# One more feed-forward layer in pairs, an earlier last chunk, and one weight sum on GpSimd

## The chip, the cores and the metric

One NeuronCore of a Trainium2 chip runs the whole network in one launch. The metric is the device time of one execution in microseconds, as the median of several runs.

## The reference

The input x is one sequence of 256 tokens with 1024 features. It passes through 13 stages: eight feed-forward layers (FFN 0 to 7) and between them four mixers (HGRN, forgetting attention, short convolution, NSA attention) and one stage that makes shared keys and values for NSA. All is float32. An FFN, which is what the change touches most, is

```python
def swiglu(h, w_in, w_out):
    gate, up = jnp.split(h @ w_in, 2, axis=-1)
    return (jax.nn.silu(gate) * up) @ w_out
# x = x + 0.5 * swiglu(rmsnorm(x), w_in, w_out), w_in 1024 x 5632, w_out 2816 x 1024
```

The shared keys and values include compressed ones: windows of 32 tokens plus a position vector, through a small two-layer network. NSA needs them, and a table of relative position biases.

## The kernel before

**Split products.** A float32 product is made of fp32r matmuls of high and low parts: hi*hi + lo*hi + hi*lo, three matmuls of 512 columns for each 128 rows of the contraction. ScalarE (ACT) makes the high part of every weight block by a copy to fp32r (lines 599, 1022, 1131), VectorE (DVE) the low part by subtracting it (lines 609, 1030, 1266). A block is 128x2048 (1 MB). TensorE (PE) does nothing but products and transposes.

**An FFN** is worked in 11 chunks of 256 hidden features (FC). For each chunk the input product (gate and up), silu and the product by DVE, a transposition of the result ("turn"), and the output product ("second"), which adds into four PSUM banks acc 0 to 3 over all chunks (bank a holds token tile a // 2, column half a % 2).

**Pairs.** In FFN 0 two and in FFN 1, 2, 3, 4 and 7 three pairs of chunks (table PAIRED, line 78; 17 pairs in all) take a Strassen-like form: seven products B11, B21, T2, T3, T1, B22, T4 of 12 matmuls each (pe_pair, line 849) in place of eight. T1 to T4 use sums of weight blocks: T3 = b12 + b22, made by a DMA of POOL's queue that adds while it loads; T2 = b11 + T3 into b11; T4 = b21 + T2 into b21; T1 = T2 - b22, over b11 (dve_block_sum, line 1033: sums at lines 1047, 1051, 1056). The last three are DVE's, and the semaphore st_add counts them in the order T2, T4, T1. Each sum is then split like any block. DVE's order in the first pair of an FFN is: split B11, output weights of the chunk before, read, turn, split B21, read, sum T2, sum T4, split T2, sum T1, split T3, split T1, split B22, split T4. In the other pairs: split B11, turn and output weights, read, sum T2, split B21, read, sum T4, split T2, sum T1, turn, output weights, split T3, and on. "Read" is silu(gate) * up (line 1332), with one operand in PSUM.

**The last chunk** (10) of an FFN: PE does second(9) in two halves, each followed by the transposes of one half of chunk 10 (line 999), and then second(10) with the half of the hidden features outside and the banks inside, so that all four banks end within the last twelve matmuls (lines 976 to 1000). ACT and DVE split its output weights into the usual tiles wo_hi and wo_lo half by half, once second(9) has freed them (lines 1237 to 1410). In paired FFNs these weights are loaded early into a place of their own (raw_last; the list ASIDE). DVE then adds the four banks to x (line 1415).

**Stage borders.** A mixer transposes x by a product with a diagonal matrix that holds 1/rms of each token: ACT squares x, DVE and ACT make the root and the reciprocal, DVE the diagonal (line 767), PE the product (line 674). An FFN after an FFN transposes x (line 676) and scales later.

**Around FFN 5.** FFN 5 is not paired; in its arena room POOL prepares the kv stage (pool_kv, line 2222): bias table, two 1 MB weight loads, and a sum over the 32 positions in 47 small instructions (line 2249), which PE uses in FFN 6 (line 2346). PE makes the product of the bias table in FFN 5 (pe_bias_slot, line 2287).

**What sets the order.** Every engine's program is written out by hand in one fixed order, with semaphores between them. SP issues the loads, in its own fixed order; a place is loaded again when the low part of what it held is made.

## Time and profile before

| what | us |
|---|---|
| median of 3 runs (2092.23 to 2093.51) | 2092.26 |
| the profiled execution, by the same clock as the runs | 2089.7 |
| span of its trace, first to last instruction | 2088.4 |
| PE busy | 2038.8 |
| DVE busy | 1512.6 |
| ACT busy | 1138.7 |
| POOL busy | 93.1 |

The mean granted TensorE clock was 0.996 of the full one. A busy share is an average over stages of different kinds; PE's ends are modelled, so its records overlap (a matmul of 512 columns has a record of 0.39 us and the next starts 0.23 later). In a timeline row, the bracket gives the idle time of the engine just before, and what ended it.

### The profile page before, as it was taken

What the parts mean: (1) busy time and instruction counts of PE and PEld (TensorE: products, weight loads), DVE (VectorE), ACT (ScalarE), POOL (GpSimd) and SP (SyncE); (2) the same over time, 40 slices, a digit from 0 to 9 for tenths busy, and PEclk for the clock granted to TensorE, in tenths of its full rate; (3) what the DMA queues carried; (4) which work ended last, traced back from release to release, by engine and by line L of the source; (5) the groups of instructions that cost most, each with busy time, mean ns of one, the idle gap of its engine ahead of it and who ended that gap; (6) DMA issues with size and microseconds to landing.
All of it is one profiled execution on the core that took longest, in us unless ns stands there. A gap on an engine that the chain in (4) does not pass through costs nothing.

```text
span 2088.4 us, 26202 instructions
## 1 busy us (share of the span) xinstructions
PE 2038.8 (98%) x10287; PEld 1705.6 (82%) x10287; DVE 1512.6 (72%) x1777; ACT 1138.7 (55%) x1417; POOL 93.1 (4%) x130
## 2 busy tenths in 40 slices
PE   8999999999999999999999999999999999989999
PEld 6887988888888778888888879888888887877887
DVE  6885687997898676698789866655555555767995
ACT  6555436555665558665566543544455444765653
POOL 2000000000000000000000000007001000000000
PEclk9999999999999999999999999999999999989999
DMA  9644426877265452687736545685637654117562
GB/s 278 237 154 150 162 82 219 259 247 241 102 222 183 143 172 73 207 260 250 238 112 211 193 141 181 194 240 185 192 131 183 202 194 164 68 42 241 182 222 81
DMA packets 232955, 377.82 MB, mean 181 GB/s; under 512 B 18766, under 2 KB 129786, under 8 KB 232832
## 3 DMA queue, kind: packets, MB, share of 16 engines
q1 hardware_dynamic: 220896, 351.56, 49.4%
q0 software_dynamic: 10992, 22.78, 6.2%
q10 hardware_dynamic: 944, 1.79, 0.3%
q8 instruction: 82, 1.34, 0.3%
q14 instruction: 41, 0.34, 0.0%
HBM read 374.53 MB, written 1.57 MB: 180 GB/s over the span
## 4 chain that ended last, share of the span: by engine, by line
PE 86%; DVE 7%; ACT 4%; issue 2%; DMA 1%; DVEq 0%; ACTq 0%; SPq 0%
PE bank L584 11%; PE bank L586 11%; PE bank L585 11%; PE acc L930 6%; PE acc L932 6%; PE acc L931 6%; PE bank L863 3%; PE bank L862 3%; PE bank L864 3%; PE tr L862 2%; PE tr L863 2%; PE bank L579 2%; PE tr L864 2%; PE bank L580 2%; PE bank L581 2%
## 5 line engine op out<-in xcount | busy, mean ns | idle before, releaser
L609 DVE TENSOR_TENSOR w_lo_<-raw_in,w_hi_ 128x2048 fp32r<-128x2048 f32 (+1 forms) x265 | 418.7, 1589 | 134.8 <-ACT w_hi_ L599 134.5
L584 PE MATMUL bank<-w_hi_,xt_hi_ 128*128 128x512 f32 x1104 | 444.1, 402 | 4.0 <-DVE xt_lo_ L710 2.4
L586 PE MATMUL bank<-w_hi_,xt_lo_ 128*128 128x512 f32 x1104 | 431.3, 391 | 0.0
L585 PE MATMUL bank<-w_lo_,xt_hi_ 128*128 128x512 f32 x1104 | 430.2, 390 | 0.0
L599 ACT ACTIVATE w_hi_<-raw_in 128x2048 fp32r<-128x2048 f32 (+1 forms) x265 | 351.2, 1346 | 76.4 <-DMA raw_in<-ffn_w_in 26.5
L1266 DVE TENSOR_TENSOR wo_lo_<-raw_out,wo_hi_ 128x2048 fp32r<-128x2048 f32 x80 | 183.5, 2293 | 195.1 <-ACT wo_hi_ L1131 195.0
L1030 DVE TENSOR_TENSOR w_lo_<-arena,w_hi_ 128x2048 fp32r<-128x2048 f32 x119 | 270.8, 2284 | 4.8 <-ACT w_hi_ L1022 4.8
L1022 ACT ACTIVATE w_hi_<-arena 128x2048 fp32r<-128x2048 f32 x119 | 225.6, 1910 | 40.8 <-DVE arena L1047 19.8
L584 PEld LDWEIGHTS bank<-w_hi_,xt_hi_ 128*128 128x128 f32 x1104 | 207.7, 188 | 45.9 <-issue 4.8
L586 PEld LDWEIGHTS bank<-w_hi_,xt_lo_ 128*128 128x128 f32 x1104 | 207.2, 188 | 44.8
L1131 ACT ACTIVATE wo_hi_<-raw_out 128x2048 fp32r<-128x2048 f32 x80 | 153.0, 1912 | 163.2 <-PE acc L932 123.1
L585 PEld LDWEIGHTS bank<-w_lo_,xt_hi_ 128*128 128x128 f32 x1104 | 208.0, 188 | 38.2
L930 PE MATMUL acc<-wo_hi_,ht_hi_ 128*128 128x512 f32 x576 | 225.5, 391 | 0.8 <-DVE ht_lo_ L1261 0.8
L932 PE MATMUL acc<-wo_hi_,ht_lo_ 128*128 128x512 f32 x576 | 224.5, 390 | 0.0
L931 PE MATMUL acc<-wo_lo_,ht_hi_ 128*128 128x512 f32 x576 | 224.2, 389 | 0.0
L930 PEld LDWEIGHTS acc<-wo_hi_,ht_hi_ 128*128 128x128 f32 x576 | 108.1, 188 | 25.1 <-issue 1.4
L932 PEld LDWEIGHTS acc<-wo_hi_,ht_lo_ 128*128 128x128 f32 x576 | 108.1, 188 | 22.7
L931 PEld LDWEIGHTS acc<-wo_lo_,ht_hi_ 128*128 128x128 f32 x576 | 108.2, 188 | 22.2
L1172 ACT ACTIVATE silu_<-bank,rstd_ 128x256 f32<-128x256 f32 x108 | 51.0, 473 | 129.2 <-PE bank L586 129.1
L1126 ACT ACTIVATE ht_hi_<-tr 128x512 fp32r<-128x512 f32 x80 | 47.5, 593 | 123.9 <-PE tr L911 110.9
L579 PE MATMUL bank<-xt_hi_,w_hi_ 128*128 128x256 f32 x352 | 101.9, 289 | 2.8 <-DVE xt_lo_ L770 2.8
L580 PE MATMUL bank<-xt_lo_,w_hi_ 128*128 128x256 f32 x352 | 99.6, 283 | 0.0
(438 smaller groups left out, 3415.0 us busy)
## 6 DMA issues: line engine op xcount, KB each, us to landing
raw_in<-ffn_w_in SPq DMA_DIRECT2D x216, 512.0 KB, 5.3
raw_out<-ffn_w_out SPq DMA_DIRECT2D x82, 1024.0 KB, 5.1
arena<-ffn_w_in SPq DMA_DIRECT2D x68, 1024.0 KB, 7.5
arena<-ffn_w_in POOLq DMA_DIRECT2D x17, 1024.0 KB, 14.0
raw_in<-hg_w_in SPq DMA_DIRECT2D x16, 1024.0 KB, 5.1
raw_in<-fox_w_in SPq DMA_DIRECT2D x16, 1024.0 KB, 5.4
raw_in<-conv_w_in SPq DMA_DIRECT2D x12, 1024.0 KB, 5.1
arena<-ffn_w_out SPq DMA_DIRECT2D x6, 1024.0 KB, 7.1
```

The lines of the kernel that those rows point to most:

```text
L584: mm(o, xt_hi[:, k, tok], wh(k)[:, 0:w], start=first, stop=False)
L585: mm(o, xt_hi[:, k, tok], wl(k)[:, 0:w], start=False, stop=False)
L586: last = mm(o, xt_lo[:, k, tok], wh(k)[:, 0:w], start=False, stop=end)
L599: act.e.activation(g.piece(g.wh, n, half, k), raw, ACT.Copy).then_inc(g.w_hi, 4 if k is None else 1)
L609: dve.e.tensor_tensor(g.piece(g.wl, n, half, k), raw, g.piece(g.wh, n, half, k).bitcast(F32), ALU.subtract).then_inc(g.w_lo, 4 if k is Non ...
L930: mm(o, g.hth[:, at, :], g.oh[:, i, cols], start=(c == 0 and i == 0), stop=False)
L931: mm(o, g.hth[:, at, :], g.ol[:, i, cols], start=False, stop=False)
L932: ins = mm(o, g.htl[:, at, :], g.oh[:, i, cols], start=False, stop=False)
L1022: act.e.activation(g.wh[:, op % 4], g.block_of(i), ACT.Copy).then_inc(g.w_hi, 4)
L1030: dve.e.tensor_tensor(g.wl[:, op % 4], g.block_of(i), g.wh[:, op % 4].bitcast(F32), ALU.subtract).then_inc(g.w_lo, 4)
L1131: act.e.activation(g.oh[:], g.raw_out[:], ACT.Copy).then_inc(g.wo_hi, 2)
L1266: dve.e.tensor_tensor(g.ol[:], g.raw_out[:], g.oh[:].bitcast(F32), ALU.subtract).then_inc(g.wo_lo, 2)
```

## The change

FFN 5 gets three pairs like FFN 1. The output weights of the last chunk are loaded in two halves into xg and a piece of the arena, and (except in FFN 6) split early into the tile that held the split sums of x. PE makes both halves' transposes after the first half of second(9), and goes through second(10) bank by bank, so that the banks end one after the other; before an FFN, the transposes of the first token tile come ahead of bank 3. DVE's additions to x are split up accordingly: before a mixer banks 2 and 3 are added behind the first diagonal. The sum T4 of each pair (b21 + T2, 128x2048) is made by GpSimd, behind its loading DMA, in place of DVE. POOL's preparation for the kv stage starts at the end of FFN 5, and the bias product moves into the kv stage.

The changed lines, cut to those that the text speaks of (the bias product's move and the last calls are left out):

```diff
@@ -75,7 +75,7 @@
-PAIRED = {f: (2, 5, 8) if f else (4, 7) for f in (0, 1, 2, 3, 4, 7)}
+PAIRED = {f: (2, 5, 8) if f else (4, 7) for f in (0, 1, 2, 3, 4, 5, 7)}
@@ -117,7 +117,7 @@
-ASIDE = [m_of(f, NCH - 1) for f in PAIRED]
+ASIDE = [m_of(f, NCH - 1) for f in range(8)]
@@ -276,11 +276,19 @@
-        self.raw_last = self.area(10240, FC // P, D)
+        self.raw_last = [self.area(8768 if f == 6 else CW, D) for f in range(8)]
-    def last_out(self, f):
-        return self.raw_last if f in PAIRED else self.raw_out
+    def last_out(self, f, i):
+        return self.raw_last[f] if i else self.xg[:].rearrange("p a b -> p (a b)")
+    def last_split(self, f):
+        if f == 6:
+            return self.oh, self.ol
+        return [self.sums_split[:, i].rearrange("p a b c -> p (a b c)").rearrange("p (i n) -> p i n", n=D)
+                for i in range(2)]
@@ -345,7 +353,7 @@
-        self.pe_w1 = [self.area(8768, 2, P), self.area(9792, 2, P)]
+        self.pe_w1 = [self.area(13120, 2, P), self.area(13376, 2, P)]
@@ -473,9 +481,13 @@
-                if f in PAIRED and c == NCH - 1:
-                    sp.wait_ge(g.prod, PDN[N0[s] + PAIRED[f][-1]] + 6)
-                    sp.e.dma_start(g.raw_last, w_out[c]).then_inc(g.last_in, 16)
+                if c == NCH - 1:
+                    if f == 6:
+                        sp.wait_ge(g.kv_hidden, 1)
+                    else:
+                        sp.wait_ge(g.prod, PDN[N0[s] + PAIRED[f][-1]] + 6)
+                    for half in range(2):
+                        sp.e.dma_start(g.last_out(f, half), w_out[c][:, half]).then_inc(g.last_in, 16)
@@ -765,6 +777,9 @@
+        if t == 0:
+            for a in (2, 3):
+                dve_ffn_add(g, dve, S_FFN.index(s - 1), a)
@@ -779,6 +794,8 @@
+            if s and STAGES[s - 1] == "ffn" and not t and not half:
+                dve_ffn_add(g, dve, S_FFN.index(s - 1), 3)
@@ -895,7 +912,7 @@
-        pe_turn_x(g, pe, s)
+        pe_turn_x(g, pe, s, first=int(s > 0 and STAGES[s - 1] == "ffn"))
@@ -973,31 +989,40 @@
-    for c in (NCH - 2, NCH - 1):
-        for i in range(FC // P):
-            if c == NCH - 2:
-                pe.wait_ge(g.ht_lo, 12 * f + c + 1)
...
+    def last_second(i, a, oh, ol, end):
+        t, cols = a // 2, slice(a % 2 * CW, (a % 2 + 1) * CW)
+        at, mm, o = i * NT + t, pe.e.matmul, g.accs[a][:]
+        mm(o, g.hth[:, at, :], oh[:, i, cols], start=False, stop=False)
+        mm(o, g.hth[:, at, :], ol[:, i, cols], start=False, stop=False)
+        return mm(o, g.htl[:, at, :], oh[:, i, cols], start=False, stop=end)
+    c = NCH - 2
+    pe.wait_ge(g.ht_lo, 12 * f + c + 1)
+    pe.wait_ge(g.wo_lo, 2 * m_of(f, c) + 2)
+    for i in range(FC // P):
+        for a in range(4):
+            ins = last_second(i, a, g.oh, g.ol, False)
+        ins.then_inc(g.second, 1)
+        if i:
+            continue
+        for t in range(NT):
+            pe.wait_ge(g.h, 22 * f + 2 * (NCH - 1) + t + 1)
+        for half in range(FC // P):
+                ins = pe.e.transpose(g.tr[half][:, t * P:(t + 1) * P], g.h_[:, t, half * P:(half + 1) * P], g.ident[:])
+    c = NCH - 1
+    oh, ol = g.last_split(f)
+    for a, i in ([(a, i) for i in range(FC // P) for a in range(4)] if f == 6 else
+                 [(a, i) for a in range(4) for i in range(FC // P)]):
+        if (a, i) == (3, 0) and s + 1 in S_FFN:
+            for half in range(2):
+                pe_turn_half(g, pe, s + 1, 0, half)
+        pe.wait_ge(g.ht_lo, 12 * f + c + i + 1)
+        pe.wait_ge(g.wo_lo, 2 * m_of(f, c) + i + 1)
+        ins = last_second(i, a, oh, ol, i == 1)
+        if i == 1:
+            ins.then_inc(g.acc, 1)
@@ -1045,10 +1070,6 @@
-    elif i == T4:
-        dve.wait_ge(g.w_lo, 4 * (op + B21) + 4)
-        dve.wait_ge(g.st_add, 3 * p + 1)
-        dve.e.tensor_tensor(b21, b21, b11, ALU.add).then_inc(g.st_add, 1)
@@ -1063,6 +1084,10 @@
+            b11, b21 = g.blocks[0], g.blocks[2]
+            pool.wait_ge(g.w_lo, 4 * (OPN[N0[S_FFN[f]] + c] + B21) + 4)
+            pool.wait_ge(g.st_add, 3 * p + 1)
+            pool.e.tensor_tensor(b21, b21, b11, ALU.add).then_inc(g.st_add, 1)
@@ -1235,13 +1260,16 @@
+    oh = g.last_split(f)[0]
+    act.wait_ge(g.last_in, 32 * (f + 1))
+    if f != 6:
+        act.wait_ge(g.prod, PDN[n0 + PAIRED[f][-1]] + 6)
+        for i in range(FC // P):
+            act.e.activation(oh[:, i], g.last_out(f, i), ACT.Copy).then_inc(g.wo_hi, 1)
-        if f in PAIRED:
-            act.wait_ge(g.last_in, 16 * (list(PAIRED).index(f) + 1))
-        else:
-            act.wait_ge(g.landed_out, 16 * outs_until(m_of(f, c)))
-        act.e.activation(g.oh[:, i], g.last_out(f)[:, i], ACT.Copy).then_inc(g.wo_hi, 1)
+        if f == 6:
+            act.e.activation(oh[:, i], g.last_out(f, i), ACT.Copy).then_inc(g.wo_hi, 1)
@@ -1355,7 +1383,6 @@
-                dve_block_sum(g, dve, p, T4)
@@ -1369,7 +1396,6 @@
-                dve_block_sum(g, dve, p, T4)
@@ -1401,19 +1427,31 @@
+    oh, ol = g.last_split(f)
+    def last_low(i):
+        dve.wait_ge(g.wo_hi, 2 * m_of(f, c) + i + 1)
+        dve.e.tensor_tensor(ol[:, i], g.last_out(f, i), oh[:, i].bitcast(F32), ALU.subtract).then_inc(g.wo_lo, 1)
+    if f != 6:
+        for i in range(FC // P):
+            last_low(i)
-        dve.wait_ge(g.wo_hi, 2 * m_of(f, c) + i + 1)
-        dve.e.tensor_tensor(g.ol[:, i], g.last_out(f)[:, i], g.oh[:, i].bitcast(F32), ALU.subtract).then_inc(g.wo_lo, 1)
+        if f == 6:
+            last_low(i)
-    for t in range(NT):
-        for half in range(2):
-            cols, a = slice(half * CW, (half + 1) * CW), 2 * t + half
-            dve.wait_ge(g.acc, 4 * f + a + 1)
-            dve.e.scalar_tensor_tensor(g.x[:, t, cols], g.accs[a][:], 0.5, g.x[:, t, cols], ALU.mult,
-                                       ALU.add).then_inc(g.x_new, 1)
+    for a in range(3 if s + 1 in S_FFN else 4 if s + 1 == len(STAGES) else 2):
+        dve_ffn_add(g, dve, f, a)
+def dve_ffn_add(g, dve, f, a):
+    t, cols = a // 2, slice(a % 2 * CW, (a % 2 + 1) * CW)
+    dve.wait_ge(g.acc, 4 * f + a + 1)
+    dve.e.scalar_tensor_tensor(g.x[:, t, cols], g.accs[a][:], 0.5, g.x[:, t, cols], ALU.mult, ALU.add).then_inc(g.x_new, 1)
@@ -1505,7 +1543,7 @@
-    pool.wait_ge(g.wo_lo, 2 * NCH)
+    pool.wait_ge(g.acc, 4)
@@ -2221,10 +2259,14 @@
-    for i in range(4):
-        pool.wait_ge(g.x_new, 4 * X[S_FFN[5] - 1] + i + 1)
+    pool.wait_ge(g.prod, PDN[N0[S_FFN[5]] + PAIRED[5][-1]] + 7)
+    pool.wait_ge(g.landed_out, 16 * outs_until(m_of(5, NCH - 2)))
+    pool.wait_ge(g.last_in, 32 * 6)
+    pool.e.dma_start(g.onehot[0:REL_ROWS], t["c_rel"]).then_inc(g.rel_in, 16)
+    for kv, w in enumerate((t["cmp_w1_k_2"], t["cmp_w1_v_2"])):
+        pool.e.dma_start(g.w1[kv * DH:(kv + 1) * DH], w.rearrange("(j d) h -> d j h", d=DH)).then_inc(g.compress_in, 16)
+    pool.wait_ge(g.acc, 4 * 6)
-    pool.e.dma_start(g.onehot[0:REL_ROWS], t["c_rel"]).then_inc(g.rel_in, 16)
@@ -2233,15 +2275,13 @@
-    for kv, w in enumerate((t["cmp_w1_k_2"], t["cmp_w1_v_2"])):
-        pool.wait_ge(g.prod, PDN[N0[S_FFN[5]] + 3 + kv])
-        pool.e.dma_start(g.w1[kv * DH:(kv + 1) * DH], w.rearrange("(j d) h -> d j h", d=DH)).then_inc(g.compress_in, 16)
+    pool.e.memset(g.kv0, 0.0).then_inc(g.kv_set, 1)
+    pool.wait_ge(g.kv_set, 6)
+    pool.e.memset(g.vv.rearrange("p a b g d -> p (a b g) d")[:, :, DH:], 1.0).then_inc(g.kv_set, 1)
+    pool.wait_ge(g.kv_set, 7)
-    pool.e.memset(g.kv0, 0.0).then_inc(g.kv_set, 1)
-    pool.wait_ge(g.kv_set, 7)
-    pool.e.memset(g.vv.rearrange("p a b g d -> p (a b g) d")[:, :, DH:], 1.0).then_inc(g.kv_set, 1)
@@ -2342,7 +2381,7 @@
-        pe.wait_ge(g.kv_set, 6)
+        pe.wait_ge(g.kv_set, 8)
@@ -3151,6 +3192,7 @@
+    pool_pairs(g, pool, 5)
```

## Rows read from the trace of the kernel before

**Rows 1.** The page's part 1: busy us, share of the span, instructions.

```profile
PE 2038.8 (98%) x10287; PEld 1705.6 (82%) x10287; DVE 1512.6 (72%) x1777; ACT 1138.7 (55%) x1417; POOL 93.1 (4%) x130
```

**Rows 2.** Waits of PE, longest kind first: total us, times, longest.

```profile
PE tr L674 <- DVE diag_ L767: 8.9, 5, 1.8
```

**Rows 3.** Timeline of PE, products B22 and T4 of FFN 1's first pair.

```profile
399.49 0.39 PE L862 MATMUL bank<-w_hi_,sums_split 128*128 128x512 f32 x1
...
402.72 0.47 PE L862 MATMUL tr<-w_hi_,xt_hi_ 128*128 128x512 f32 x1 [0.28 <-DVE w_lo_ L1030]
```

**Rows 4.** Timeline of PE, FFN 1 and FFN 5: start us, us, instruction.

```profile
354.22 0.38 PE L676 MATMUL tr<-ident,x_tok 128*128 128x128 f32 x2
...
535.64 0.39 PE L990 MATMUL acc<-wo_hi_,ht_lo_ 128*128 128x512 f32 x1
...
1339.83 0.38 PE L676 MATMUL tr<-ident,x_tok 128*128 128x128 f32 x2
...
1528.97 0.39 PE L990 MATMUL acc<-wo_hi_,ht_lo_ 128*128 128x512 f32 x1
```

**Rows 5.** The chain that ended last, near 1349: start us, us, what.

```profile
1348.65 0.96 PE acc L2292 x2
```

**Rows 6.** Timeline of POOL, where the sum over positions begins.

```profile
1412.19 0.61 POOL L2254 TENSOR_TENSOR arena<-arena,gains 128x256 f32<-128x256 f32 x1 [9.25 <-DMA arena<-cmp_w_v]
```

**Rows 7.** Timeline of DVE, then of POOL, near 1448.

```profile
1448.08 2.72 DVE L609 TENSOR_TENSOR w_lo_<-raw_in,w_hi_ 128x2048 fp32r<-128x2048 f32 x1 [0.68 <-ACT w_hi_ L599]
...
1448.04 0.61 POOL L2254 TENSOR_TENSOR arena<-arena,gains 128x256 f32<-128x256 f32 x1
1448.73 2.39 POOL L2261 TENSOR_TENSOR arena<-arena 128x128 f32<-128x128 f32 x1
```

**Rows 8.** Timeline of PE, the product with the sum over positions.

```profile
1591.89 0.28 PE L2346 MATMUL acc<-arena 128*128 128x2 f32 x2
```

**Rows 9.** Timeline of DVE, then of PE, from FFN 0 into the mixer.

```profile
194.63 1.38 DVE L1415 SCALAR_TENSOR_TENSOR x_tok<-acc,x_tok 128x512 f32<-128x512 f32 x2 [1.05 <-PE acc L990]
...
198.42 0.35 PE L674 MATMUL tr<-diag_,x_tok 128*128 128x128 f32 x1 [1.78 <-DVE diag_ L767]
```

**Rows 10.** Timeline of DVE, then of ACT, first pair of FFN 1.

```profile
383.22 2.29 DVE L1051 TENSOR_TENSOR arena<-arena 128x2048 f32<-128x2048 f32 x1
385.43 2.28 DVE L1030 TENSOR_TENSOR w_lo_<-arena,w_hi_ 128x2048 fp32r<-128x2048 f32 x1
...
396.21 2.28 DVE L1030 TENSOR_TENSOR w_lo_<-arena,w_hi_ 128x2048 fp32r<-128x2048 f32 x1
...
383.21 1.92 ACT L1022 ACTIVATE w_hi_<-arena 128x2048 fp32r<-128x2048 f32 x1 [2.81 <-DVE arena L1047]
```

**Rows 11.** Groups of POOL by form: count | busy us, mean ns | idle before.

```profile
L3003 POOL TENSOR_TENSOR arena<-silu_ 128x128 f32<-128x128 f32 x16 | 7.3, 456 | 264.1 <-DVE silu_ L2913 264.1
...
L2283 POOL COPY arena<-arena 128x240 f32<-128x240 f32 x1 | 0.6, 607 | 0.0
...
L2283 POOL COPY arena<-arena 128x112 f32<-128x112 f32 x1 | 0.4, 382 | 18.0 <-DMA arena<-bias_rows 18.0
```

**Rows 12.** Timeline of DVE, second pair of FFN 1, then of FFN 2.

```profile
423.58 2.28 DVE L1030 TENSOR_TENSOR w_lo_<-arena,w_hi_ 128x2048 fp32r<-128x2048 f32 x1
...
428.38 2.28 DVE L1030 TENSOR_TENSOR w_lo_<-arena,w_hi_ 128x2048 fp32r<-128x2048 f32 x1
...
433.56 2.28 DVE L1266 TENSOR_TENSOR wo_lo_<-raw_out,wo_hi_ 128x2048 fp32r<-128x2048 f32 x1
...
614.82 2.28 DVE L1266 TENSOR_TENSOR wo_lo_<-raw_out,wo_hi_ 128x2048 fp32r<-128x2048 f32 x1
```

**Rows 13.** Timeline of PE, where each of those two output parts is used.

```profile
437.02 0.40 PE L930 MATMUL acc<-wo_hi_,ht_hi_ 128*128 128x512 f32 x1
...
618.69 0.40 PE L930 MATMUL acc<-wo_hi_,ht_hi_ 128*128 128x512 f32 x1
```

More of the change, by code:

```diff
@@ L677, in pe_turn_half, with pe_turn_x @@
     ins.then_inc(g.turned, 1)
-def pe_turn_x(g, pe, s):
-    for t in range(NT):
+def pe_turn_x(g, pe, s, first=0):
+    for t in range(first, NT):
         for half in range(2):
@@ L914, in second @@
     def second(c):
-        if c == 0 and f == 5:
+        if c == 0 and f == 6:
             pe.wait_ge(g.kv_rows, 1)
-        elif c == 0 and f == 6:
             pe.wait_ge(g.kv_gelu, 2)
@@ L998, in pe_ffn @@
-            for t in range(NT):
-                ins = pe.e.transpose(g.tr[i][:, t * P:(t + 1) * P], g.h_[:, t, i * P:(i + 1) * P], g.ident[:])
+                ins = pe.e.transpose(g.tr[half][:, t * P:(t + 1) * P], g.h_[:, t, half * P:(half + 1) * P], g.ident[:])
             ins.then_inc(g.h_turned, 1)
+    c = NCH - 1
[10 more added lines that the diff above has]
+            ins.then_inc(g.acc, 1)
@@ L2319, in pe_kv @@
             j = 2 * (c - 1) + t
+            if (c, t) == (1, 0):
+                pe_bias(g, pe)
             if c == 1:
@@ L2366, in read @@
                 return
+            if j == 0:
+                act_bias(g, act)
             if j == 3:
@@ L3100, in pe_program @@
     pe_conv(g, pe)
[L3101 removed]
+    pe_ffn(g, pe, 5)
     pe_kv(g, pe)
```

48 lines of the change are left out of this document (13 added, 35 removed).

## Prediction

> **What bounds the kernel now.** I read the page's busy times first: PE is busy for 2038.8 us of a span of 2088.4 [rows 1]. So all stalls of TensorE together are worth at most 50 us, and a change can win in two ways only: less work for PE, or fewer of those stalls. Then the waits of PE: the largest regular one is at the start of each mixer, where the transposes wait for the diagonal matrix, 8.9 us in five waits [rows 2]. Last the timelines of one FFN, engine by engine. There VectorE (DVE) runs almost without a gap from the split of one weight block to the next, and it comes in just ahead of PE: in the first pair PE already waits 0.28 us for a weight split [rows 3]. What matters for the moved sum is therefore not how much DVE does, but how far ahead of PE each of its splits is.
>
> The profiled execution took 2089.7 us, 2.6 below the median of the three runs (2092.26). I make the sum against the profiled execution and add it to the median.
>
> **Part 1, FFN 5 in pairs.** FFN 1, which has three pairs and also follows a mixer, runs from 354.22 to 535.64 + 0.39 = 536.03, or 181.8 us; FFN 5 without pairs runs from 1339.83 to 1528.97 + 0.39 = 1529.36, or 189.5 us [rows 4]. The difference is 7.7 us. The count agrees: a pair needs 7 x 12 matmuls where two plain chunks need 96, so 3 x 12 = 36 fewer at about 0.23 us each, 8.3 us, less what the pair form loses. The bias product (0.96 us [rows 5]) now sits in FFN 5 and only moves to the kv stage. Term: -7.7 + 0.96 = **-6.8 us**.
>
> What moves with it: POOL's preparation for the compressed keys. Its position sum ran from 1412 [rows 6] to past 1448 [rows 7], some 40 us. Its two 1 MB weight loads now go out near the end of FFN 5, its memsets and two small loads behind the last accumulation, 1529 less 7. Fifteen us for memsets and loads and 40 for the sum end some 7 us before the product that needs it, which came at 1591.89, 62.5 us behind FFN 5's end [rows 8]. I cost it at nothing; if the sum is 15 us longer, the kernel pays 8. The small adds also hold DVE's splits of the kv stage by up to 0.44 us each, as they held those of FFN 5 before, where no wait of PE came of it. SP's block loads and POOL's three more accumulating loads in FFN 5 follow the order of FFN 1, whose stretch contains them.
>
> **Part 2, the last chunk and the stage borders.** The weights of the last chunk are split before the chunk, and the accumulators end one after the other, so the additions to x start sooner. Before, PE stood 1.78 us at a mixer's start [rows 9]: the last addition (0.7, half of the pair of 1.38 [rows 9]) and the chain of statistics to the diagonal (1.1). After, tile 0's diagonal is ready when PE ends. But DVE adds the last two quarters only behind that diagonal, so tile 1's comes two additions (1.4), a square on ScalarE (0.8, an estimate from the additions, of the same size) and the 1.1 later, 3.2 us behind PE's end, where its transposes used to start at 1.78 plus tile 0's own, about 1.95. That wins 0.5 a border. It gives back 0.2, because the second half of the last chunk's activations is now needed after three matmuls instead of twelve. Four borders at -0.3; at the NSA stage FFN 6 keeps its order and only gets the later additions (+0.8); two FFN-FFN borders at -0.1; the end of the kernel, where the last addition follows the same +0.2, +0.3. Term: -1.2 + 0.8 - 0.2 + 0.3 = **-0.3 us**. Nothing in the rows shows this order, so the ends are -5 (most of the 8.9 gone) and +3.
>
> **Part 3, the fourth sum on GpSimd.** It goes from DVE, where it took 2.29 us [rows 10], to POOL, 20 times (17 pairs before, three more in FFN 5). Two things follow: its own length P, and what DVE does meanwhile.
>
> The length. No such add is in the trace. POOL's add of 128 columns took 456 ns; its copies of 112 and 240 columns took 382 and 607 [rows 11], which is 1.76 ns a column above a fixed 0.185. A multiplication of 256 columns with a repeated second operand took 0.61 [rows 6]. Low end: the step from 456 to 610 carried on, 2.8 us. High end: 16 x 456, 7.3 us, as if nothing of an instruction were fixed. The copy's line with a second input can't be under 3.8. I take the add's own row with the copy's fixed part, (456 - 185) / 128 = 2.12 ns a column, so **P = 4.5 us**. The Trainium skill (GPSIMD Engine Reference, section 3.1) gives a measured 4497 ns for this very add and tells authors to leave two-input arithmetic to VectorE; by that figure the sum would be the same.
>
> What DVE does. At 1448.04 a POOL multiply starts; DVE's split starts 0.04 later and takes 2.72 us instead of 2.28; POOL's next add, from 1448.73, takes 2.39 instead of 0.46 [rows 7]. I read this as exclusion: whichever engine started first with two SBUF inputs, the other stood. Then DVE is held not for 0.44 but for all of P. The Trainium skill (SBUF — State Buffer, "Who interferes with whom") says so: an instruction of VectorE with two SBUF inputs and a GpSimd instruction that reads SBUF exclude each other for the whole instruction. The trace shows it only for POOL operations of half a us. With that rule the sum is the one below; without it, it is rival (a).
>
> First pair of an FFN. The fourth sum started at 383.22, right behind the second; ScalarE made the high part of that same second sum in its shadow (383.21, 1.92 us), and DVE's split of it came at 385.43 [rows 10]. After, POOL starts at 383.2, surely first, since DVE has nothing to do until 385.1, and DVE's split starts at 383.3 + P: later by P - 2.13, 2.4 us. Everything DVE does up to the split of B22 follows back to back. That split ended at 396.21 + 2.28 = 398.49 and PE wanted it at 399.49 [rows 3, 10]: 1.0 us is covered. The 0.28 us wait at the next product goes, since its chain starts at PE itself. Loss P - 3.4 = 1.1 us, in seven FFNs (0 to 5 and 7): **+7.6 us**.
>
> Second pair (chunk 5). POOL starts behind the split of B21 (423.58 + 2.28), while DVE reads a PSUM bank, and is ahead again. DVE's next split, at 428.38, starts at 426.05 + P, 2.2 us late. The split of the output weights ended at 433.56 + 2.28 = 435.84, and PE wanted it at 437.02; in FFN 2 at 617.10 and 618.69 [rows 12, 13]. Covered are 1.2 and 1.6 us, so the loss is 1.0 and 0.6, mean 0.85, in six FFNs (1 to 5 and 7): **+5.1 us**. Both losses together grow by 13 us for each us of P: at the high end of 7.3 they would be 49 us, at the low end of 2.8 they are nothing, or at best the seven waits of 0.28 less, -2 us. In the third pair the same split lies further ahead of PE, and I take nothing. DVE's third sum overwrites what the fourth reads and so waits for POOL as well; with the split held, that wait is over when DVE comes to it. SP and POOL: the fourth sum queues behind the accumulating load of its own pair, long landed, and ahead of the next pair's, whose target is not loaded before the third product's split; I take nothing.
>
> **Sum:** -6.8 - 0.3 + 7.6 + 5.1 = **+5.6 us**, 0.27%: 2095.3 for the profiled execution, 2097.9 for the median.
>
> **Rivals.** (a) *Faster: no exclusion over the whole length.* If DVE passes beside a long POOL add, its split runs at 385.1, and only the third sum waits for POOL, until 387.8 at P = 4.5, when it began anyway (385.43 + 2.28). Then part 3 costs nothing and the time is 2092.3 - 7.1 = 2085.2. It decides at the split behind the second sum: 2.3 us long under this rival, about 4.9 under mine. Against it: the 2.72 us [rows 7]. (b) *The add is short.* Exclusion holds but P is 3.8 or less: the losses fall to 0.4 and 0.15 a pair, 3.7 us in all, and the time is 2088.9. Part 3 costs nothing below P = 3.4. (c) *The losses are larger:* P = 5.3 adds 0.8 us to 13 pairs, 10.4 us, 2108; a position sum that holds up the kv stage or FFN 6 would end near there too. (d) *The change doesn't do what it says:* both calls on DVE are gone and FFN 5 is in the table of pairs, so this isn't open; what could be is that FFN 5 gains less, because its block loads meet POOL's 2 MB; that is 1 to 3 us inside the ranges.
>
> **Chances.** My case (P of 4.2 to 4.8, full exclusion) 0.55; (a) 0.15; (b) or losses half as large as read 0.15; (c) 0.15. A change of 0.2%, 4.2 us, is what a measurement of this kernel can tell from none. My own case has its losses known to about 3 us, so it ends above 2096.5 in two of three, and within 0.2% else. Slower 0.48, within 0.2% 0.27, faster 0.25. The range takes in (a) and (c): 2084 to 2108; my case alone is 2094 to 2102.
>
> **What would show it.** In the profile after: POOL rows for a 128x2048 add, 20 of them, near 4.5 us; the split behind the second sum near 4.9 us in first pairs and as long in second pairs; new waits of PE for a weight split (about 1 us, at the products T3 and B22 of first pairs) and for the output weights' low part in second pairs; FFN 5 about 7 us shorter; the waits for the diagonal split into a small one and one of about 1.2 us. If the split stays at 2.3 us, my reading of the exclusion is wrong and the kernel is faster; if POOL's add is 3 us, the price was.

## The result, and the profile after

The changed kernel takes 2111.7 us (median of 4 runs, 2109.1 to 2117.4) against 2092.2 for the kernel before beside it: a ratio of 1.0099, with an interval of [1.0087, 1.0111]. It is slower by 19.5 us. The prediction was 2097.9, between 2084 and 2108. The sign was right, the size was not: 19.5 where 5.6 was forecast, and outside the range.

The profiled execution took 2109.1 us. First the page's part 1 of the changed kernel, to be read against [rows 1]:

```profile
PE 2040.4 (97%) x10251; PEld 1700.7 (81%) x10251; DVE 1586.2 (75%) x1792; ACT 1158.1 (55%) x1421; POOL 186.3 (9%) x153
```

PE has 36 matmuls fewer, as counted. DVE has lost the 2.3 us sum in 17 pairs, and yet it is busy for 74 us more. A part is the work of FFN 5's pairs (run 1 below, without the move, has 1566 us); the rest is time in which DVE's instructions were held, and their records count it as busy. It shows in the groups of instructions, whose columns are the form, the count, the busy time, the mean length in ns, and the idle time before:

```profile
L1055 DVE TENSOR_TENSOR w_lo_<-arena,w_hi_ 128x2048 fp32r<-128x2048 f32 x140 | 384.2, 2752 | 27.3 <-ACT w_hi_ L1047 27.3
...
L1090 POOL TENSOR_TENSOR arena<-arena 128x2048 f32<-128x2048 f32 x20 | 92.3, 4614 | 514.4 <-DVE w_lo_ L1055 261.9 <-DVE arena L1072 252.5
```

GpSimd's sum takes 4.6 us, twenty times. The weight splits of the pairs, which took 2.28 us [rows 10, 12], now take 2.75 in the mean: if 120 of them are as before, the 20 beside POOL's sum are longer by 3.2 us each. In the timeline they are 4.8 us in first pairs, 6.2 to 6.5 in second pairs and 5.1 in third pairs (6.5 in FFN 2's); the prediction had put the second pairs at 4.9 like the first. The waits of PE (total us, times, longest), longest kind first:

```profile
PE bank L879 <- DVE silu_ L1303: 9.4, 7, 2.1
PE tr L928 <- DVE ht_lo_ L1289: 9.2, 8, 1.8
PE acc L686 <- DVE diag_ L779: 6.8, 5, 2.1
```

The first two are new. They are 18.6 us, and PE's idle time as a whole grew by 18 us. Neither is the wait whose cover I had computed (at the product of B22, and at the output weights). My list of signs had named the product T3 too, but for a weight split, not for a read of DVE.

### The profile page after: what moved, and what is told of

It is laid out like the page before. It is cut to its first block, busy times and chain, and to the rows that moved or that the text cites. A ratio compares the mean times of both kernels' runs of the same rounds, so it can differ in the third digit from the quotient of the medians.

```text
span 2107.7 us, 26229 instructions
## 1 busy us (share of the span) xinstructions
PE 2040.4 (97%) x10251; PEld 1700.7 (81%) x10251; DVE 1586.2 (75%) x1792; ACT 1158.1 (55%) x1421; POOL 186.3 (9%) x153
## 4 chain that ended last, share of the span: by engine, by line
PE 80%; DVE 10%; ACT 6%; issue 3%; DMA 0%; DVEq 0%; ACTq 0%; SPq 0%
PE bank L596 10%; PE bank L598 10%; PE bank L597 10%; PE acc L946 6%; PE acc L948 6%; PE acc L947 6%; DVE w_lo_ L1055 3%; PE bank L879 2%; PE bank L880 2%; PE bank L881 2%; PE bank L591 2%; PE tr L879 2%; PE bank L592 2%; PE bank L593 2%; PE tr L880 2%
## 5 line engine op out<-in xcount | busy, mean ns | idle before, releaser
L621 DVE TENSOR_TENSOR w_lo_<-raw_in,w_hi_ 128x2048 fp32r<-128x2048 f32 (+1 forms) x247 | 390.4, 1589 | 128.6 <-ACT w_hi_ L611 128.2
L596 PE MATMUL bank<-w_hi_,xt_hi_ 128*128 128x512 f32 x1008 | 406.2, 403 | 3.8 <-DVE xt_lo_ L722 2.0
L1055 DVE TENSOR_TENSOR w_lo_<-arena,w_hi_ 128x2048 fp32r<-128x2048 f32 x140 | 384.2, 2752 | 27.3 <-ACT w_hi_ L1047 27.3
L598 PE MATMUL bank<-w_hi_,xt_lo_ 128*128 128x512 f32 x1008 | 393.9, 391 | 0.0
L597 PE MATMUL bank<-w_lo_,xt_hi_ 128*128 128x512 f32 x1008 | 392.8, 390 | 0.0
L611 ACT ACTIVATE w_hi_<-raw_in 128x2048 fp32r<-128x2048 f32 (+1 forms) x247 | 327.8, 1347 | 80.5 <-DMA raw_in<-ffn_w_in 31.1
L1047 ACT ACTIVATE w_hi_<-arena 128x2048 fp32r<-128x2048 f32 x140 | 265.6, 1911 | 74.3 <-DVE arena L1077 46.5
L598 PEld LDWEIGHTS bank<-w_hi_,xt_lo_ 128*128 128x128 f32 x1008 | 189.1, 188 | 41.0
L1090 POOL TENSOR_TENSOR arena<-arena 128x2048 f32<-128x2048 f32 x20 | 92.3, 4614 | 514.4 <-DVE w_lo_ L1055 261.9
L947 PEld LDWEIGHTS acc<-wo_lo_,ht_hi_ 128*128 128x128 f32 x576 | 108.2, 188 | 22.2
L879 PE MATMUL bank<-w_hi_,sums_split 128*128 128x512 f32 x240 | 96.9, 404 | 9.4 <-DVE silu_ L1303 9.4
```

The costliest lines, as they stand in the source:

```text
L596: mm(o, xt_hi[:, k, tok], wh(k)[:, 0:w], start=first, stop=False)
L597: mm(o, xt_hi[:, k, tok], wl(k)[:, 0:w], start=False, stop=False)
L598: last = mm(o, xt_lo[:, k, tok], wh(k)[:, 0:w], start=False, stop=end)
L611: act.e.activation(g.piece(g.wh, n, half, k), raw, ACT.Copy).then_inc(g.w_hi, 4 if k is None else 1)
L621: dve.e.tensor_tensor(g.piece(g.wl, n, half, k), raw, g.piece(g.wh, n, half, k).bitcast(F32), ALU.subtract).then_inc(g.w_lo, 4 if k is Non ...
L879: mm(bank[:], hi[:, k], wh[:, k], start=k == 0, stop=False)
```

## Where the held split lands

The first pair of FFN 1, DVE, then POOL, then PE (start us, us, instruction):

```profile
384.36 2.28 DVE L1072 TENSOR_TENSOR arena<-arena 128x2048 f32<-128x2048 f32 x1
388.76 4.82 DVE L1055 TENSOR_TENSOR w_lo_<-arena,w_hi_ 128x2048 fp32r<-128x2048 f32 x1 [2.12 <-ACT w_hi_ L1047]
...
398.08 0.69 DVE L1303 TENSOR_TENSOR silu_<-bank,arena 128x512 f32<-128x512 f32 x1
```
```profile
386.80 4.63 POOL L1090 TENSOR_TENSOR arena<-arena 128x2048 f32<-128x2048 f32 x1 [16.75 <-DVE arena L1072]
```
```profile
398.82 0.50 PE L879 MATMUL bank<-w_hi_,sums_split 128*128 128x512 f32 x1 [1.23 <-DVE silu_ L1303]
399.15 0.40 PE L880 MATMUL bank<-w_lo_,sums_split 128*128 128x512 f32 x1
```

The split is held until POOL is through and then runs: 4.82 us, where I had said 4.9. Everything behind it on DVE is late, and PE stops at the T3 product. This product writes PSUM bank 1, and may do so only when DVE has read the second product out of it. That read is the addition at L1303 (`gate0` in the code), queued behind the split of T3. In the kernel before, the same read and the first matmul of T3 stood like this, DVE and PE:

```profile
392.21 0.69 DVE L1275 TENSOR_TENSOR silu_<-bank,arena 128x512 f32<-128x512 f32 x1
...
393.89 0.39 PE L862 MATMUL bank<-w_hi_,sums_split 128*128 128x512 f32 x1
```

The read ended at 392.90, 1.0 us ahead of PE. This time by which an instruction is ahead of whoever needs it is its cover.

The second pair, DVE, POOL, PE:

```profile
428.42 2.28 DVE L1055 TENSOR_TENSOR w_lo_<-arena,w_hi_ 128x2048 fp32r<-128x2048 f32 x1
...
431.02 6.52 DVE L1055 TENSOR_TENSOR w_lo_<-arena,w_hi_ 128x2048 fp32r<-128x2048 f32 x1
437.63 2.29 DVE L1077 TENSOR_TENSOR arena<-arena 128x2048 f32<-128x2048 f32 x1
439.84 0.68 DVE L1289 TENSOR_TENSOR ht_lo_<-tr,ht_hi_ 128x512 fp32r<-128x512 f32 x1
440.44 2.28 DVE L1294 TENSOR_TENSOR wo_lo_<-raw_out,wo_hi_ 128x2048 fp32r<-128x2048 f32 x1
```
```profile
430.79 4.60 POOL L1090 TENSOR_TENSOR arena<-arena 128x2048 f32<-128x2048 f32 x1 [20.11 <-DVE w_lo_ L1055]
```
```profile
440.58 0.66 PE L928 MATMUL tr<-ident,h_tok 128*128 128x128 f32 x4 [1.60 <-DVE ht_lo_ L1289]
```

PE stops for 1.60 us at the transposes of the middle chunk. They overwrite the bank from which DVE takes the low half of the hidden rows turned before (ht_lo), 0.6 us of work that stands behind the T1 sum. In the kernel before, the T1 sum, ht_lo and the turn stood like this:

```profile
430.75 2.29 DVE L1056 TENSOR_TENSOR arena<-arena 128x2048 f32<-128x2048 f32 x1
432.96 0.68 DVE L1261 TENSOR_TENSOR ht_lo_<-tr,ht_hi_ 128x512 fp32r<-128x512 f32 x1
...
433.79 0.60 PE L911 MATMUL tr<-ident,h_tok 128*128 128x128 f32 x4
```

ht_lo ended at 433.64 and PE turned at 433.79: a cover of 0.15 us. I had read the cover from the next instruction of DVE, the output weights' low part, where it was 1.2. DVE itself came as late as forecast: from the split of B21 to the T1 sum it took 430.75 - 423.58 = 7.17 us before [rows 12] and 437.63 - 428.42 = 9.21 after, 2.0 us more (2.2 forecast).

Two of the eight waits at the turn lie in pairs that the prediction had at nothing, FFN 0's second pair and FFN 2's third:

```profile
129.14 0.66 PE L928 MATMUL tr<-ident,h_tok 128*128 128x128 f32 x4 [1.78 <-DVE ht_lo_ L1289]
...
674.57 0.66 PE L928 MATMUL tr<-ident,h_tok 128*128 128x128 f32 x4 [0.94 <-DVE ht_lo_ L1289]
```

There the cover before was 1.35 and 2.75 us, so 2.0 us alone do not explain them. But DVE entered these two pairs already late against PE, by 1.2 and 1.7 us more than in the kernel before (start of its T2 sum against PE's B11 product): what PE does not wait for in one pair is still owed in the next. In the other pairs that both kernels have, this carried delay is 0.3 us or less.

## Experiments

Each run is given with its median, its ratio to the kernel before and the interval of that ratio; the medians of the kernel before beside them were 2091.3 to 2091.9. An interval reaches 0.8 to 1.4 thousandths to either side, 1.8 to 2.9 us, so a difference between two runs of less than some 3 us is not shown by the medians.

**1. The sum back on VectorE** (the changed kernel, one part undone):

```diff
+    elif i == T4:
+        dve.wait_ge(g.w_lo, 4 * (op + B21) + 4)
+        dve.wait_ge(g.st_add, 3 * p + 1)
+        dve.e.tensor_tensor(b21, b21, b11, ALU.add).then_inc(g.st_add, 1)
...
-            pool.e.tensor_tensor(b21, b21, b11, ALU.add).then_inc(g.st_add, 1)
```

> The changed kernel with one part undone: VectorE makes the fourth weight sum of each pair again. **Theory A** (GpSimd's 4.6 us sum holds VectorE's next instruction from start to end, and TensorE pays for that at the second product of the first pairs and at the turn of the second pairs): counted from the gaps of the changed kernel's trace, the sum costs some 22 us in seven FFNs, so this kernel takes 2111.7 - 22 = 2090 us, 2086 to 2094. **Rival B** (the other parts, the pairing of FFN 5 and the borders, are what lost the time): 2105 us or more. The first pair of FFN 1 should show the second product's wait of 1.2 us gone.

2088.3 us, 0.9982 [0.9974, 0.9991]. So the moved sum costs 23.4 us (2111.7 against 2088.3), and all the rest of the change wins 3.6. The wait at L879 for DVE's addition is gone.

**2. Only the sum moved** (the kernel before, with the POOL call in and the two DVE calls out):

> The kernel before with only the fourth weight sum moved to GpSimd, in its 17 pairs (FFN 5 stays unpaired). **Theory A**: the 22 us without the 2.8 us of FFN 5, so +19 us: 2092.2 + 19 = 2111 us, 2107 to 2115. **Rival B**: under 2098 us. If the sum of the two single changes (this one against before, the other against before) is the whole change, the parts don't touch one another.

2114.1 us, 1.0103 [1.0089, 1.0116]: +22.2 us for 17 pairs, 3 more than expected. With run 1's -3.6 and the 2.8 us that I had counted for FFN 5's pairs, the two single changes make +21.4, against +19.5 for the whole: additive as far as the intervals can tell. Its trace has the same two new waits, at the same places, and something on top, told in the last section:

```profile
PE tr L911 <- DVE ht_lo_ L1261: 8.5, 7, 2.7
PE bank L862 <- DVE silu_ L1275: 8.1, 6, 1.9
```

**3. The turn ahead of the T1 sum** (the changed kernel):

```diff
-            dve_block_sum(g, dve, p, T1)
             turn(pending)
+            dve_block_sum(g, dve, p, T1)
             weights_out(pending)
```

> The changed kernel with one order turned round on VectorE: in the second and third pair of an FFN it makes the low half of the turned hidden rows (0.6 us) ahead of the T1 sum (2.2 us), not behind it. **Theory A**: the wait of TensorE at the turn of the middle chunk (1.6, 1.6, 1.2, 1.1, 0.9, 0.3, and 1.8 in FFN 0, 0.9 in FFN 2's third pair: 9.3 us in sum) needs that low half and goes: 2111.7 - 9.3 = 2102.4 us. **Rival C** (VectorE's whole row of work is late by the held 4.2 us, and what is moved ahead only makes the T1 block later): the wait comes back at the T1 product, and the time stays within 3 us of 2111.7.

2103.9 us, 1.0057 [1.0043, 1.0071]: 7.8 us less for 0.6 us of work moved ahead of 2.2. PE's turn in FFN 1 no longer waits; its next stop is the one that the prediction had named for second pairs:

```profile
437.53 0.60 PE L928 MATMUL tr<-ident,h_tok 128*128 128x128 f32 x4
...
441.61 0.50 PE L946 MATMUL acc<-wo_hi_,ht_hi_ 128*128 128x512 f32 x1 [0.68 <-DVE wo_lo_ L1294]
```

**4. One column instead of 2048** (the changed kernel):

```diff
-            pool.e.tensor_tensor(b21, b21, b11, ALU.add).then_inc(g.st_add, 1)
+            pool.e.tensor_tensor(b21[:, 0, 0:1], b21[:, 0, 0:1], b11[:, 0, 0:1], ALU.add).then_inc(g.st_add, 1)
```

> The changed kernel with GpSimd's fourth weight sum cut to one column of 2048 (the rest of the block stays B21, so T4 is wrong in the output): the hand-over from VectorE to GpSimd to ScalarE stays, the 4.6 us of GpSimd work go. **Theory A** (the length of the held time is what costs): all of the 22 us go, about as with the sum on VectorE, 2088 to 2091 us. **Rival D** (the hand-over between the engines, or the order of VectorE's work, is what costs): 2105 us or more. The difference to the run with the sum on VectorE is what freeing VectorE of 2.2 us in each pair is worth by itself; I expect under 1 us of it.

2087.8 us, 0.9977 [0.9968, 0.9986]. The hand-over between the engines costs nothing that can be told; the length of POOL's work is what costs. It also prices what was to be won: VectorE freed of 2.3 us in every pair is worth 0.6 us against run 1, which these runs can't tell from nothing.

**5. The same time on GpSimd without a read** (the changed kernel):

```diff
-            pool.e.tensor_tensor(b21, b21, b11, ALU.add).then_inc(g.st_add, 1)
+            pool.wait_ge(g.own_pool, pool.step(pool.e.memset(b21, 0.01)))
+            pool.wait_ge(g.own_pool, pool.step(pool.e.memset(b21, 0.01)))
+            pool.e.memset(b21[:, 0:2], 0.01).then_inc(g.st_add, 1)
```

(The waits on `own_pool` only put the fills one behind the other.)

> The changed kernel with GpSimd's fourth weight sum replaced by two fills of the whole block and one of its half with a constant (T4 is that constant, so the output is wrong): GpSimd works in the same place about as long (a fill of 128x2048 took 1.81 us in the changed kernel's trace, so some 4.5 us in sum), but reads nothing from SBUF. **Theory A1** (VectorE's instructions with two SBUF inputs are held only by a GpSimd instruction that reads SBUF): the splits in the pairs keep their 2.3 us, and what is left is that T4 comes 4.5 us after B21: 2088 to 2091 us, near the small add's 2087.8. **Rival E** (any long GpSimd instruction holds them): near the changed kernel's 2111.7. The Trainium skill (SBUF, on the shared port pair) states the first; it also lets a fill hold a one-input instruction in its fast mode, which would agree with the diagonal of the kv stage that took 1.20 us beside a fill.

2088.3 us, 0.9982 [0.9973, 0.9991]. POOL works for 4.7 us in the same place and DVE's split beside it keeps its length. POOL and DVE, first pair of FFN 1:

```profile
383.75 1.82 POOL L1090 MEMSET arena<- 128x2048 f32 x1 [16.66 <-DVE arena L1072]
385.63 1.81 POOL L1091 MEMSET arena<- 128x2048 f32 x1
387.50 0.95 POOL L1092 MEMSET arena<- 128x1024 f32 x1
```
```profile
385.75 2.29 DVE L1055 TENSOR_TENSOR w_lo_<-arena,w_hi_ 128x2048 fp32r<-128x2048 f32 x1 [2.12 <-ACT w_hi_ L1047]
388.58 2.29 DVE L1077 TENSOR_TENSOR arena<-arena 128x2048 f32<-128x2048 f32 x1 [0.54 <-POOL arena L1092]
...
431.42 2.29 DVE L1077 TENSOR_TENSOR arena<-arena 128x2048 f32<-128x2048 f32 x1 [2.31 <-POOL arena L1092]
```

So the exclusion is between a VectorE instruction with two SBUF inputs and a GpSimd instruction that reads SBUF. The Trainium skill (SBUF — State Buffer, "Who interferes with whom") states this rule, and the trace agrees, at 4.6 us as at half a us. That one with a single SBUF input passes is shown only for a short stretch: in the changed kernel DVE's read of a bank at L1360 keeps its 0.48 us with the last 0.3 of it beside POOL's add. The later T4 leaves a trace in the third sum, which overwrites an input of T4 and so waits for POOL: 0.5 us in first pairs, 2.3 in second (the last row, FFN 1) and 0.8 in third pairs. That is no more than the 2.3 us that DVE gave away. Only in FFN 7 does PE wait more than in run 1, 0.9 us at the turn for 0.5, and 0.2 at T3.

**6. Half of the block** (`b21[:, 0:2]` and `b11[:, 0:2]`, in run 4's place):

> The changed kernel with GpSimd's fourth weight sum cut to half of the block (128x1024; the other half stays B21, so T4 is wrong there): GpSimd's instruction then takes about 2.3 us. **Theory A** (what counts is the held time beyond the 2.2 us that VectorE saved by giving the sum away, and beyond the slack of its next product): held some 1.9 us, so VectorE is as late as in the kernel with the sum on VectorE: nearly all of the 22 us go, 2088 to 2092 us. **Rival H** (the loss is in proportion to GpSimd's time): half of it stays, about 2100 us.

2087.6 us, 0.9977 [0.9967, 0.9986]. POOL's instruction takes 2.4 us and the loss is not half but nothing that can be told. The price is not in proportion to POOL's time, since DVE gave away 2.3 us of its own:

```profile
L1090 POOL TENSOR_TENSOR arena<-arena 128x1024 f32<-128x1024 f32 x20 | 48.0, 2399 | 528.7 <-DVE w_lo_ L1055 272.5 <-DVE arena L1072 256.2
```

**7. GpSimd's sum in all but the first pairs** (run 3's kernel; DVE makes it where `c == PAIRED[f][0]`):

> The kernel with the turn ahead of the T1 sum (2103.9 us), and the fourth sum back on VectorE in the first pair of each of the seven FFNs; GpSimd makes it in the 13 others. **Theory A** (each first pair loses 1.2 us at its T3 product, which waits for VectorE's gate in the queue behind the held instruction, and 0.2 to 0.3 at T4): 7 x 1.5 = 10.5 us go, 2103.9 - 10.5 = 2093.4 us, 2091 to 2096; what is left over 2088.3 are the waits of the second pairs at the low half of their output weights, 0.7 us in FFN 1. **Rival I** (T4's price in the first pairs is only the 0.2 us at T4, and the loss lies elsewhere): above 2100 us.

2092.0 us, 1.0003 [0.9994, 1.0012]: 11.9 us less than run 3 (11.4 if each is set against the kernel before beside it), so the seven first pairs cost 1.6 to 1.7 each. What is left over run 1 is 3.6 us, and its trace shows it in the second pairs, at the output weights. With the turn out of the way it is the wait of the prediction, 0.65 to 0.93 us in five of the FFNs, where I had forecast 0.85 in six:

```profile
PE acc L947 <- DVE wo_lo_ L1303: 4.1, 5, 0.9
```

**8. FFN 5 unpaired again** (run 1's kernel; the waits that named FFN 5's third pair name its chunk 8 instead):

```diff
-PAIRED = {f: (2, 5, 8) if f else (4, 7) for f in (0, 1, 2, 3, 4, 5, 7)}
+PAIRED = {f: (2, 5, 8) if f else (4, 7) for f in (0, 1, 2, 3, 4, 7)}
```

> The kernel with the sum back on VectorE (2088.3 us), and FFN 5 unpaired again; the last chunk's order and the borders stay as changed. It prices the pairing of FFN 5, which I put at -6.8 us, and with it the bias product moved into the kv stage. **Theory A**: 2088.3 + 6.8 = 2095 us, 2093 to 2097, so that the borders alone cost about 3 us against the kernel before. **Rival F** (the pairing brought only what the whole of the first try shows, and the borders nothing): 2092 us.

2096.2 us, 1.0021 [1.0012, 1.0029]. The pairing wins 7.8 us. But what is left of the change without it and without the moved sum is 4.5 us slower than the kernel before, and I had put that at -0.3.

**9. The fill of kv0 a little later** (run 1's kernel):

```diff
     pool.wait_ge(g.kv_set, 5)
+    pool.wait_ge(g.xt_lo, 16 * U[S_KV] + 1)
     pool.e.memset(g.kv0, 0.0).then_inc(g.kv_set, 1)
```

> The kernel with the sum back on VectorE, and GpSimd's fill of kv0 (1.81 us) held until the first low half of the kv stage's turned rows is made, so that it no longer lies beside VectorE's second diagonal (1.20 us in the changed kernel, 0.29 without a fill beside it). **Theory A**: the diagonal takes 0.29 us again and TensorE's gap of 2.09 us there becomes 1.2: 2088.3 - 0.9 = 2087.4 us, which the comparison can only just tell; the trace's gap is the measure. **Rival G** (the gap is set by ScalarE's row sums, not by the diagonal's length): the gap stays at 2 us.

2084.9 us, 0.9970 [0.9958, 0.9981]: 3.5 us less than run 1, where 0.9 was expected. DVE and POOL at the start of the kv stage, first in run 1's kernel, then here:

```profile
1525.84 1.20 DVE L779 TENSOR_SCALAR diag_<-ident,rstd_ 128x128 f32<-128x128 f32 x1
...
1525.16 1.81 POOL L2280 MEMSET arena<- 128x2048 f32 x1
```
```profile
1525.29 0.29 DVE L779 TENSOR_SCALAR diag_<-ident,rstd_ 128x128 f32<-128x128 f32 x1
...
1525.96 1.81 POOL L2281 MEMSET arena<- 128x2048 f32 x1 [1.41 <-DVE xt_lo_ L785]
```

The diagonal is 0.9 us shorter, and the gap of PE behind it 1.2 us instead of 2.1. Behind the longer gap, run 1's profiled execution also shows a lower clock. The columns of its windows are the length, the busy time of each engine, then the granted clock of PE, the DMA share and GB/s:

```profile
1525.50:1527.00 1.50, 0.00 (x0) 0.00 (x0) 1.32 (x3) 0.36 (x2) 1.47 (x1) 1.00 0.00 0
1527.00:1530.50 3.50, 3.30 (x15) 3.33 (x16) 0.05 (x2) 0.00 (x0) 1.28 (x4) 0.52 0.09 26
```

0.52 is about the lower level, 1.2 GHz, and the 16 transposes took 1.6 us longer than at 1.00. In this execution that makes 2.5 us together. But of the eight kernels with the fill in the old place only four show longer transposes in their profiled execution (last section), 0.6 us in the mean of all eight. So some 1.5 us of the 3.5 have a place; the rest is inside the intervals.

**10. The same in the kernel of run 8**:

> The kernel with FFN 5 unpaired and the sum on VectorE (2096.2 us, 4.5 over the kernel before, where I had put the borders at -0.3), with GpSimd's fill of kv0 held back as in the run that took 2084.9 us. **Theory A** (the borders as such are worth nothing either way, and the loss there is the fill beside the diagonal and what follows from it, 3.5 us): 2092.7 us, 2091 to 2094. **Rival K** (the 3.5 us had their place only in the paired FFN 5, or were chance, and the borders themselves lose 4 us): 2095.5 us or more.

2094.4 us, 1.0013 [1.0005, 1.0022]: only 1.8 us less than run 8, which the medians can't tell from nothing, and 3.0 still over the kernel before. The result lies between the two theories, nearer to rival K: the fill is not the whole of the loss.

**11. The borders alone** (the kernel before, with only the new order of the last chunk and of the borders; the last chunks of FFN 5 and 6 and the kv stage as before):

> The kernel before with only the new order of the last chunk and of the borders (in FFN 5 and 6 the last chunk's splits stay as they were); FFN 5, the loads of w1, the bias product, the position sum and the fill of kv0 lie where they lay before. **Theory A** (the borders as such are worth about nothing, as the prediction's -0.3 had it; the 3.0 us that the run with the later fill was still over the kernel before come from what moved into the kv stage, the bias product and the position sum, and from a clock that fell for longer): 2091.5 us, 2090 to 2093. **Rival K** (the new border order itself loses about 1 us at the three borders where TensorE now waits between the two halves of the turn): 2094 us or more.

2095.0 us, 1.0015 [1.0006, 1.0024]: +3.2 us, as rival K had it in size. Its place was to be the mixer borders. PE where FFN 6 meets the NSA stage, before and in this run:

```profile
1773.08 2.02 PE L674 MATMUL tr<-diag_,x_tok 128*128 128x128 f32 x16 [1.78 <-DVE diag_ L767]
1775.30 0.91 PE L674 MATMUL acc<-diag_,x_tok 128*128 128x128 f32 x6 [0.20 <-DVE diag_ L767]
```
```profile
1776.73 2.02 PE L686 MATMUL tr<-diag_,x_tok 128*128 128x128 f32 x16 [1.43 <-DVE diag_ L779]
1779.93 1.24 PE L686 MATMUL acc<-diag_,x_tok 128*128 128x128 f32 x9 [1.18 <-DVE diag_ L779]
```

The gaps are 0.6 us more there, and 0.8 more at the kv stage, whose FFN also kept its old last chunk here. Not at the borders behind a new last chunk, though, and so rival K's place is wrong. Set side by side by the start of the first product of each stage, the profiled executions of this run and of the kernel before are level up to FFN 5 (1342.8 and 1343.0 us), so five new last chunks with three mixer and two FFN borders neither win nor lose. Then this run falls back by 1.1 us up to FFN 6 (1565.2 and 1564.3), and by 3.7 more up to the product behind the NSA border (1781.7 and 1777.1). In FFN 6 lie a longer wait and a lower clock, told in the last section.

**12. The old additions behind the old last chunks** (run 11's kernel; all four additions to x go ahead of the statistics at the kv and the NSA stage):

```diff
-    for a in range(3 if s + 1 in S_FFN else 4 if s + 1 == len(STAGES) else 2):
+    for a in range(3 if s + 1 in S_FFN else 4 if s + 1 == len(STAGES) or f in (5, 6) else 2):
...
-        if t == 0:
+        if t == 0 and s not in (S_KV, S_NSA):
             for a in (2, 3):
```

> The kernel with the borders alone (2095.0 us), with all four additions ahead of the statistics again at the two borders behind an FFN with the old last chunk, kv and NSA. **Theory A** (in the trace the gaps there grew by 0.8 and 0.6 us, the others did not): 2095.0 - 1.4 = 2093.6 us. **Rival L** (what follows from those gaps, a longer wait of FFN 6 and the lower clock behind it, goes with them): 2091.8 us, no more than the kernel before. **Rival M** (the loss is not at these borders): 2095 us.

2092.9 us, 1.0009 [1.0000, 1.0017]: 1.6 us over the kernel before are left of the 3.2. The half that went is about theory A's 1.4, and the gaps are 1.78 us again, but the interval reaches down to rival L and overlaps that of run 11, so the median rules out neither L nor M.

**13. The same at the NSA stage alone**, on run 9's kernel:

> The best version so far (sum on VectorE, later fill in kv, 2084.9 us), with all four additions to x ahead of the statistics again where FFN 6 meets the NSA stage, because FFN 6 kept its old last chunk. TensorE stood 1.43 + 1.18 us there in the changed kernel and 1.78 + 0.20 in the kernel before. **Theory A** (the late additions pay only where the last chunk frees the accumulators one by one): 2084.9 - 0.6 = 2084.3 us, and the two gaps become 1.78 and 0.20; so small a step shows in the gaps, not in the medians. **Rival L** (the whole loss of the borders, 3.2 us, sits at such borders): up to 1.6 us less, 2083.3.

2085.3 us, 0.9973 [0.9962, 0.9983]: the gap is 1.78 again and the median is that of run 9, as far as it can be told.

**14. GpSimd's sum in the third pairs alone** (with the order of run 3 and the fill of run 9):

> The kernel with the later fill in kv (2084.9 us), GpSimd making the fourth sum only in the six third pairs, and the turn ahead of the T1 sum in second and third pairs. It tests the step of the prediction that the third pairs cost nothing. **Theory A** (there ScalarE's high half of T2 comes 1.4 us after VectorE is ready, and the turn is covered): within 1.5 us of 2084.9, so it still beats the kernel before by some 7 us. **Rival J** (a held instruction costs everywhere): 6 x 1.5 = 9 us more, 2094 us.

2085.7 us, 0.9972 [0.9961, 0.9984], 0.8 us from run 9: with the turn made first, third pairs cost nothing that can be told. In the changed kernel's own order one of them did, FFN 2's 0.94 us.

The version to keep is run 9: VectorE makes the sum, FFN 5 is paired, the fill of kv0 waits. It beats the kernel before by 0.3% and the changed one by 1.3%; runs 13 and 14 equal it.

## Why the prediction failed

| part | predicted | measured | from runs |
|---|---|---|---|
| FFN 5 in pairs | -6.8 | -7.8 | 8, 1 |
| last chunk, borders, what moved into kv | -0.3 | +4.5 | 8 |
| of this, the order of the borders | -0.3 | +3.2 | 11 |
| fourth sum on GpSimd | +12.7 | +23.4 | 1 |
| of this, first pairs | +7.6 | +11.9 | 7, 3 |
| of this, second and third pairs | +5.1 | +11.5 | the rest |
| sum | +5.6 | +19.5 | |

That the three parts add up to +20.1 is no check: each is the difference from one kernel to the next, from the kernel before to the changed one. The check that they don't depend on one another is run 2.

**Right.** The length of the sum, 4.5 us predicted from a row of 128 columns and 4.6 measured. The exclusion over the whole length: rival (a) falls with the 4.8 us of the held split, (b) with the row of POOL; run 5 shows what (a) would have been worth. The delay of DVE. The position sum at nothing: no wait of PE names it. The pairing within 1 us. At the three mixer borders behind a new last chunk, the wait for the diagonal became one of 1.18 us and a small one of 0.23 for 1.78, as forecast.

**The step that failed** is the cover in the second pairs: "Covered are 1.2 and 1.6 us, so the loss is 1.0 and 0.6". The delay on DVE was right, 2.0 us measured for 2.2. But I asked only when PE wants what DVE *writes*. ht_lo, one instruction ahead of the output weights on DVE, is also a *read*, of the bank which PE's next turn overwrites. Its cover was 0.15 us in FFN 1. Run 3 shows it: turned round, the waits at the turn shrink from 9.2 to 0.6 us and the loss at the output weights appears, 0.4 to 0.9 us in four FFNs, of the size forecast or less.

Two more terms of that step were put at nothing. FFN 0's second pair was left out without a reason (20 sums were moved and 13 pairs priced), and it has the longest of these waits, 1.78 us. The third pairs were left out because their split lies further ahead of PE, and FFN 2's lost 0.94. In both, the sum took every pair to begin level, while DVE carried a delay over from the pair before.

**The first pairs** had the wrong instruction and were sized too small, 1.1 us each for 1.6 to 1.7. The same kind of reader was overlooked: the addition at L1303 frees bank 1 for the T3 product. Its cover happened to be the 1.0 us that I had read at B22, so PE waited 1.23, where I had forecast 1.1. The 0.28 at T4 did not go either; it is still 0.2. And a wait costs more than its idle time. Idle time is counted from the end of the last record, 0.16 us behind the point where the next matmul would have started (0.39 less 0.23), and the first matmul behind the wait took 0.50 us and the next began 0.33 later, not 0.23. That is 1.5 us for an idle time of 1.23. FFN 7's first pair waited 2.1; why its wait is longer no run shows. The seven cost 11.9 us (run 7), not 7.6. With the same surplus of some 0.2 us at each turn, the 18.6 us of new waits come to some 22 of the 23.4.

**The borders** came out 4.8 us worse than forecast, and not where the forecast had its terms: the mixer borders went as read, and the NSA stage got +0.8, against 0.6 in the gaps. I had no row for the kv stage's fill, which now lay beside a diagonal, and had listed the memsets only as work that ends in time. The rest of run 11's +3.2 lies in FFN 6 in its profiled execution, where the prediction had no term: a wait of 1.97 us for 0.80 and a lower clock behind it. Whether this belongs to the new order stays open, since run 2, which has the old order, lost 2.7 us in FFN 6 too.

The range missed because case (c) priced losses that are larger only through P or through the position sum, not through a smaller cover. The covers were read with an error of one instruction, and each tenth of a us counts up to twenty times.

## What to carry to other kernels

- When an engine falls behind, follow every instruction in its queue, and for each ask two things: who needs what it writes, and who waits to overwrite what it reads. The shorter of the two is the cover. What the cover hides is carried on: count the engine's delay into the next round before reading the next cover.
- In these runs a GpSimd instruction that reads SBUF held VectorE's splits and sums (two SBUF inputs) until it ended, for 2.7 to 4.4 of its 4.6 us. Moving such work is harmless here up to the length that VectorE gives away: 2.4 us for 2.3 cost nothing that can be told, 4.6 us cost 23 us a kernel.
- Ask first what the freed engine is worth. Here run 4 says 0.6 us, so that the move could lose 20 and win nothing.
